# Attention on one core in steps of two heads, with four context rows weighted on TensorE in each step

## The chip, the cores and the metric

The kernel runs on 1 core of one Trainium2 chip. The metric is the device time of the program in microseconds (us). The engines of the core work side by side and are joined by semaphores: TensorE (PE), VectorE (DVE), ScalarE (ACT), GpSimd (POOL) and SyncE (SP).

## What is computed

The program is one inference step of two layers (`DEPTH` 2) with 128 context tokens and 512 latent tokens of width 1024, all in float32. Cut to what the change touches, a layer of the reference is:

```python
# latent tokens: 16 query heads in 4 key/value heads, keys = 512 latent + 128 cached
q, k = axial_rope(rms_norm(aq), rows), axial_rope(rms_norm(ak), rows)
p = softmax(einsum('bqkgd,bskd->bkgqs', q, [k, ctx_k]) * ATTN_SCALE)
o_att = einsum('bkgqs,bskd->bqkgd', p, [v, ctx_v])
y = (sigmoid(ga) * (o_rec @ w_branch_rec) + sigmoid(gb) * (o_att @ w_branch_att)) @ w_out
x = layer_norm(ALPHA * x + g1 * y)

# PEER: each token has 8 x 16 = 128 experts of 16384, chosen by top-k
a   = gelu(einsum('td,thkd->thk', h2, u_tab[expert]))      # 128 dot products a token
out = einsum('thk,thkd->td', gate * a, v_tab[expert])      # 128 weighted rows a token
x = layer_norm(ALPHA * x + g2 * out)
```

`o_rec` is a gated linear recurrence (HGRN) of 8 heads. Context and latent tokens go through the same layer with the same weights. The 128 context tokens are one tile, the 512 latent tokens are four.

## The kernel before

**Stages.** Each layer runs: the context pass (tile 0) up to its own PEER choice (`one_mix(ctx_tile)`); the gate projections of the latent tokens; 8 HGRN heads; the key, value and query projections; attention; `one_mix(one_tile)`, which is the branch mix, first norm and PEER choice of latent tile 1; the mix of the other three latent tiles; and PEER of the four latent tiles. Weight blocks of 2 MB come over the SP queue into the two slots of `ring`, in the fixed order of a list.

**Context PEER runs beside the latent work.** A PEER row is one expert of each of the 128 tokens, gathered from the table by an indirect DMA that POOL issues (L368): 128 partitions of 1024 floats, 512 KB. The context tile has 128 rows of `u` (dot products, L1879 on DVE, each with a sum over its 1024 products) and 128 rows of `v` (weighted sums, L1884 on DVE, into two partial sums that `merge_sums` joins). POOL issues them in order into 8 slots (`grow`); a slot is free when DVE is done with its row. `ctx_rows(count)` takes the next rows of this list wherever DVE's program calls it: 24 in the gate stage (`GATE_ROWS`), 6 in each HGRN head, one behind each of the levels 1 to 6 of 7 (`HEAD_ROWS`, called at L1987), 22 and 4 in the key and query stage, 2 in each attention unit, and what is left of the 256 inside `one_mix(one_tile)` (L1906).

**Attention** is 64 units a layer: 8 pairs of heads (`att_pair`), and in each pair the two heads by four tiles of 128 queries. Per unit PE computes scores of 128 queries and 640 keys (`score`, L1321 and L1322, from 64 partitions, since a head has 64 dimensions); DVE takes the minimum over the keys (`lowest`, L2078; the sign is turned); ACT takes the exponential with the row sum (L702); PE transposes the 640 probabilities in five blocks (`turn`, L1331); ACT copies them out (L717); PE multiplies by the values (`weigh`, L1347, five matmuls of 128 columns, the 64 value columns twice). Once a pair, POOL stages the queries (L377), PE transposes them (L1312), DVE divides by the row sums (`normalise`), and PE turns the result (L1355). In the first pair DVE also norms and rotates the second half of the query heads (`head_norm`, seven parts).

**Order.** Nothing reorders instructions: each engine runs its program as it is written, so the place of a call in the code is its place in the queue. PE waits at `claim` (L816) for a bank of PSUM or at semaphores. In the trace a float32 matmul stands as two instructions, a transpose as one.

**HGRN heads.** Each head goes through 7 levels; in each, DVE multiplies (L1625, L1626), copies, places a score by a mask (L1616) and takes a context row; PE waits for `level_ready`. Behind the levels DVE scales the gates of the next head (`decays`, L1959 and L1960).

## Time and profile before

| what | us |
|---|---|
| time, median of 3 runs (lowest, highest) | 5605.55 (5605.12, 5608.3) |
| span of the profiled execution | 5604.2 |
| PE busy | 4557.5 |
| DVE busy | 3712.8 |
| POOL busy | 2184.8 |
| ACT busy | 1424.7 |
| weighted context rows on DVE (L1884) | 318.8 |
| context dot rows on DVE (L1879) | 308.5 |

The profiled execution's span is 1.35 us below the median. Busy time is the sum of the instructions of an engine; engines overlap, so the sums say how full an engine is and not what sets the end. For that the stages are looked at one by one: a window is a stretch of the span, and its row gives the busy time of each engine in it, the TensorE clock that was granted as a share of full speed, and what the DMA engines moved. The attention of layer 0 lies from 888.70 to 1170.04 us, of layer 1 from 3671.02 to 3952.99 us, and `one_mix(one_tile)` follows each.

### The profile page before, as it was taken

Reading aid. Unit: us, or ns where it says so; the run is one execution under the profiler, and the core shown is the slowest. Engines: PE = TensorE matmul, PEld = TensorE weight load, DVE = VectorE, ACT = ScalarE, POOL = GpSimd, SP = SyncE. Lnnn points to the kernel's source line nnn. Section 1 sums busy time; section 2 is a strip of 40 time slices with the busy share of each in tenths; the row PEclk is TensorE's granted clock in tenths of the full one; section 3 lists DMA queues with packets and bytes.
Section 4 is the critical chain, followed back from the end, with each engine's and each line's share of the span. In section 5 each row is a group of like instructions: output and inputs, shape, how many; then the busy total and the mean of one; then the engine's idle time right before and its main releaser. Section 6 shows DMA issues by size and latency. Waiting matters only on the chain. (4 is left out here: it accounts for less than half of the span.)

```text
span 5604.2 us, 60591 instructions
## 1 busy us (share of the span) xinstructions
PE 4557.5 (81%) x17704; PEld 2520.6 (45%) x17704; DVE 3712.8 (66%) x7028; ACT 1424.7 (25%) x3646; POOL 2184.8 (39%) x1826
## 2 busy tenths in 40 slices
PE   7889988888676777777787999888795878777776
PEld 6556655646343322222265566556463433223222
DVE  2357768867788766754532677788677877677545
ACT  2112213411011333333321112134100113333333
POOL 0002124642656454455400121246336554444554
PEclk9999998999888999999999999989897989999999
DMA  7755336785989999999967543457869889999998
GB/s 267 266 184 194 122 131 219 255 331 215 384 318 346 421 419 418 418 421 416 383 225 275 197 163 117 175 191 254 330 243 365 326 311 421 421 419 411 421 421 345
DMA packets 296082, 1703.74 MB, mean 304 GB/s; under 512 B 33360, under 2 KB 43216, under 8 KB 175696
## 3 DMA queue, kind: packets, MB, share of 16 engines
q0 software_dynamic: 258048, 1342.29, 61.3%
q1 hardware_dynamic: 23712, 338.18, 15.8%
q10 hardware_dynamic: 14000, 19.42, 1.0%
q8 instruction: 148, 2.42, 0.2%
q14 instruction: 174, 1.43, 0.1%
HBM read 1694.52 MB, written 5.24 MB: 303 GB/s over the span
## 5 line engine op out<-in xcount | busy, mean ns | idle before, releaser
L368 POOL DMA_INDIRECT arena<-in_peer_uv,eidx x1024 | 1184.3, 1157 | 1458.7 <-POOLq L367 1195.4
L2151 DVE SCALAR_TENSOR_TENSOR arena<-arena 128x1024 f32<-128x1024 f32 x384 | 470.6, 1225 | 349.9 <-DMA arena<-in_peer_uv,eidx 338.4
L861 PE MATMUL banks<-arena 128*128 128x512 f32 x896 | 502.1, 643 | 237.7 <-PEq L1473 234.2
L411 POOL DMA_INDIRECT arena<-in_peer_uv,eidx x384 | 490.3, 1277 | 501.0 <-POOLq L410 475.7
L863 PE MATMUL banks<-arena 128*128 128x512 f32 x896 | 477.8, 616 | 0.0
L834 PE MATMUL banks<-ring,arena 128*128 128x512 f32 x864 | 383.7, 599 | 110.0 <-PEq L816 110.0
L463 ACT ACTIVATE arena<-arena 128x1 f32<-128x1 f32 (+1 forms) x772 | 156.9, 203 | 1035.4 <-ACTq L462 1033.6
L861 PEld LDWEIGHTS banks<-arena 128*128 128x128 f32 x896 | 155.3, 198 | 549.7 <-issue 549.2
L468 ACT ACTIVATE arena<-ident,arena 128x128 f32<-128x128 f32 x832 | 333.6, 401 | 234.7 <-ACTq L467 230.2
L2151 DVE SCALAR_TENSOR_TENSOR ring<-ring,arena 128x1024 f32<-128x1024 f32 x192 | 235.4, 1226 | 211.1 <-DMA ring<-in_peer_uv,eidx 209.9
L2161 DVE SCALAR_TENSOR_TENSOR arena<-arena 128x1024 f32<-128x1024 f32 x256 | 306.9, 1225 | 95.3 <-DMA arena<-in_peer_uv,eidx 80.8
L354 POOL COPY eidx<-arena 128x128 uint32<-128x128 uint32 x8 | 2.7, 338 | 939.8 <-POOLq L353 939.8
L1159 PE MATMUL banks<-hT,ring 128*128 128x512 f32 x768 | 350.4, 595 | 0.8 <-PEq L816 0.8
L1884 DVE SCALAR_TENSOR_TENSOR arena<-arena 128x1024 f32<-128x1024 f32 x256 | 318.8, 1283 | 42.8 <-DMA arena<-in_peer_uv,eidx 29.9
L1879 DVE SCALAR_TENSOR_TENSOR arena<-arena 128x1024 f32<-128x1024 f32 x256 | 308.5, 1227 | 46.8 <-DMA arena<-in_peer_uv,eidx 22.5
L411 POOL DMA_INDIRECT hT<-in_peer_uv,eidx x192 | 233.3, 1215 | 267.3 <-POOLq L410 251.0
L411 POOL DMA_INDIRECT ring<-in_peer_uv,eidx x192 | 261.1, 1360 | 176.4 <-POOLq L410 151.6
L861 PE MATMUL banks<-hT,arena 128*128 128x512 f32 x384 | 215.3, 643 | 140.7 <-PEq L1473 140.1
L2151 DVE SCALAR_TENSOR_TENSOR hT<-hT,arena 128x1024 f32<-128x1024 f32 x192 | 235.4, 1226 | 136.9 <-DMA hT<-in_peer_uv,eidx 127.6
L834 PE MATMUL banks<-ring,hT 128*128 128x512 f32 x672 | 304.9, 614 | 22.1 <-PEq L816 20.0
L834 PEld LDWEIGHTS banks<-ring,arena 128*128 128x128 f32 x864 | 161.9, 191 | 321.6 <-issue 321.5
L863 PEld LDWEIGHTS banks<-arena 128*128 128x128 f32 x896 | 177.8, 198 | 229.1 <-issue 229.1
(303 smaller groups left out, 7763.1 us busy)
## 6 DMA issues: line engine op xcount, KB each, us to landing
ring<-in_wblk SPq DMA_DIRECT2D x160, 2048.0 KB
arena<-in_peer_uv,eidx POOLq DMA_INDIRECT x1408
arena<-in_lnrows ACTq DMA_DIRECT2D x6, 1024.0 KB, 9.5
arena<-in_sk ACTq DMA_DIRECT2D x4, 1024.0 KB, 7.4
hT<-in_peer_uv,eidx POOLq DMA_INDIRECT x192
ring<-in_peer_uv,eidx POOLq DMA_INDIRECT x192
x<-in_x_sample ACTq DMA_DIRECT2D x1, 2048.0 KB, 28.6
out<-arena ACTq DMA_DIRECT2D x4, 512.0 KB, 7.5
```

The source lines that it names most:

```text
L368: nc.gpsimd.indirect_dma_start(grow[j], None, ins["peer_uv"], bass.IndirectOffsetOnAxis(ap=eidx[:, n, r:r + 1].bitcast(U32), axis=0)).then ...
L411: nc.gpsimd.indirect_dma_start(gslot[j], None, ins["peer_uv"].rearrange("(e h) d -> e (h d)", h=2), bass.IndirectOffsetOnAxis(ap=eidx[:, n ...
L463: return nc.scalar.activation(av[:, first:last], av[:, first:last], ACT.Gelu)
L468: nc.scalar.activation(diag[n], ident[:], ACT.Copy, scale=weight).then_inc(diag_ready, 1)
L834: last = nc.tensor.matmul(banks[:, b, :], lhs[:, k, t * P:(t + 1) * P], ring[:, s, k, :], start=k == 0, stop=k == KD - 1)
L861: nc.tensor.matmul(banks[:, b, :], diag[n], row[:, 0:CB], start=start, stop=stop, skip_group_check=True).then_inc(diag_used, 1)
L863: nc.tensor.matmul(banks[:, b + 1, :], diag[n], row[:, CB:D], start=start, stop=stop, skip_group_check=True).then_inc(free, 1)
L1159: last = nc.tensor.matmul(banks[:, 4 + c, :], ring[:, s, k, c * P:(c + 1) * P], hT[:, k, :], start=k == 0, stop=k == KD - 1)
L1879: V.scalar_tensor_tensor(grow[j], grow[j], 1.0, h2c, ALU.mult, ALU.mult, accum_out=av[:, r:r + 1]).then_inc(row_free[j], 1)
L1884: V.scalar_tensor_tensor(sums[r % 2], grow[j], wv[:, r - SLOTS:r - SLOTS + 1], sums[r % 2], ALU.mult, ALU.add).then_inc(row_free[j], 1)
L2151: V.scalar_tensor_tensor(u, u, 1.0, h2[:, t - 2, :], ALU.mult, ALU.mult, accum_out=av[:, r:r + 1])
L2161: V.scalar_tensor_tensor(grow[j], grow[j], 1.0, h2c, ALU.mult, ALU.mult, accum_out=av[:, r:r + 1]).then_inc(row_free[j], 1)
```

## The change

**Attention steps.** A step `n` is a pair of heads and one tile of 128 queries; there are 32 a layer. Both heads' scores lie in banks 0 to 3, one operation takes the minimum of both (a 128x2x640 view), and the probabilities of both are turned in three portions of 4, 4 and 2 blocks through bank 4. `weigh` puts the values first and the probabilities second, so that the result comes out turned, in two tiles of 64 columns of the array; two more matmuls spread the reciprocals of the row sums, and one multiplication (L2236) finishes the step. POOL's staging of queries is gone; PE turns one query block in each step.

**Context rows on TensorE.** The weighted sums of context rows (L1884 and `merge_sums`) are gone from DVE. In step `n` PE runs `ctx_group(n)`: four rows, each a matmul of 32 stationary columns with 512 moving columns for each half of the row, in the four column tiles of the array, 8 matmuls in all, with sums in banks 6 and 7. For this the context tokens are laid out anew: partition 32a+t and row 32j+q hold another expert of the tokens than before, so the expert numbers, gates and `h2c` are permuted by small copies (`ctx_ids`, 16 a half on DVE; 16 on ACT at the start of the key and query stage) and by `replicate` (8 times four DMAs on ACT's queue). DVE makes the diagonal weights of 16 rows in one multiplication (`spread_weights`, 128x512, 8 a layer).

**Rows and slots.** Dot rows have 6 slots (3 from row 96 on), weighted rows 7, of which four are in ring slot 1; POOL issues in each step first dot rows, then four weighted rows. SP holds the next load into ring slot 1 until PE has run group 31. Dot rows: 16 in the gate stage, 7 in a head (one behind level 0 too), 22 and 4, and 30 in the first 13 steps. `one_mix(one_tile)` has no row left.

**Smaller moves.** The scaling in `decays` moves to ACT (`keys_in`). The norm of the second query half goes in two batches of 4 heads, in steps 0 to 6 and 9 to 15, one part in a step. Gelu comes in two halves.

Core of the diff:

```diff
-GATE_ROWS = 24
-HEAD_ROWS = 6
+GATE_ROWS = 16
+HEAD_ROWS = 7
-UNIT_ROWS = 2
+STEP_ROWS = [3] + [2] * 6 + [3] * 2 + [2] * 3 + [3]
+DOT_SLOTS, LATE_SLOTS, SUM_SLOTS = 6, 3, [3, 4, 5, 12, 13, 14, 15]
...
+                    if n == len(CTX_BLOCKS + LAT_BLOCKS) + 1:
+                        assert n % 2 == 1
+                        sp.wait_ge(ring_given, 1)
+                        sp.sem_inc(ring_given, -1)
                     load(n % 2, l * NB + b)
...
+            def ctx_rows_in():
+                dot_rows(0, dots_end + LATE_SLOTS)
+                pool.wait_ge(ring_idle, 1)
+                pool.sem_inc(ring_idle, -1)
+                sum_rows(0, len(SUM_SLOTS))
+                dots, sums = dots_end + LATE_SLOTS, len(SUM_SLOTS)
+                for n in range(1, STEPS):
+                    last = min(SLOTS, dots_by(n) + LATE_SLOTS)
+                    dot_rows(dots, last)
+                    dots, last = last, min(SLOTS, len(SUM_SLOTS) + REPS * n)
+                    sum_rows(sums, last)
+                    sums = last
...
+                def ctx_group(q):
+
+                    if q % BUILD == 0:
+                        pe.wait_ge(blocks_ready, 1)
+                        pe.sem_inc(blocks_ready, -1)
+                    weights = blocks[q // BUILD % 2].rearrange("p (q j t) -> p q j t", q=BUILD, j=REPS)
+                    for j in range(REPS):
+                        r = REPS * q + j
+                        pe.wait_ge(row_full[row_slot(1, r)], landed[l, 1, r])
+                    for half in range(2):
+                        for j in range(REPS):
+                            slot = row_slot(1, REPS * q + j)
+                            op = nc.tensor.matmul(banks[32 * j:32 * j + 32, 6 + half, :], weights[:, q % BUILD, j, :],
+                                                  row_buf[slot][:, half * CB:(half + 1) * CB],
+                                                  start=q == 0, stop=q == QG - 1, skip_group_check=True)
+                            if half:
+                                op.then_inc(row_free[slot], 1)
...
+                for n in range(STEPS):
+                    for half in range(2):
+                        pe.wait_ge(prob_ready[half], 1)
+                        pe.sem_inc(prob_ready[half], -1)
+                    turn(n, 0, 4)
+                    if n + 1 < STEPS:
+                        score(n + 1)
+                    turn(n, 4, 8)
+                    if n:
+                        weigh(n - 1)
+                    if n + LT in (4 * LT, 6 * LT):
+                        pe.wait_ge(qn_ready, 1)
+                        pe.sem_inc(qn_ready, -1)
+                    turn(n, 8, 10)
+                    ctx_group(n)
+                pe.drain().then_inc(ring_given, 1)
...
-                        if tl is one_tile:
-                            ctx_rows((2 * SLOTS - jobs["at"] + 3 - n) // (4 - n))
...
-                        V.tensor_scalar(keys, keys, omlb[:, n:n + 1], None, ALU.mult)
-                        V.tensor_scalar(keep, keep, omlb[:, n:n + 1], lbf[:, n:n + 1], ALU.mult, ALU.add)
...
+                    V.tensor_reduce(low[n % 2], both_scores, AX.X, ALU.min).then_inc(low_ready[0], 1)
...
+                for n in range(STEPS):
+                    if n + 1 < STEPS:
+                        lowest(n + 1)
+                    invert(n)
+                    if n:
+                        finish(n - 1)
```

On PE, before, a unit is L1331 (turn), L1321 and L1322 (score) and L1347 (weigh); in unit 5 of the first pair L1312, which turns the next pair's queries, stands between:

```order
L1331 MATMUL banks<-ident,arena 128x128 x5
L1321 MATMUL banks<-arena 128x512
L1322 MATMUL banks<-arena 128x128
L1312 MATMUL banks<-ident,arena 128x128 x4
L1347 MATMUL banks<-arena 128x128 x5
```

And one step of the changed kernel, the second (L1433 turns, L1423 and L1425 score, L1450 weighs, L1455 spreads reciprocals, L1436 turns queries, L1472 is the context group, with rows in `arena` or `ring`):

```order
L1433 MATMUL banks<-ident,arena 128x128 x4
L1423 MATMUL banks<-arena 128x512 x2
L1425 MATMUL banks<-arena 128x128 x2
L1433 MATMUL banks<-ident,arena 128x128 x4
L1450 MATMUL banks<-arena 64x128 x10
L1455 MATMUL banks<-ident,small 64x128 x2
L1433 MATMUL banks<-ident,arena 128x128 x2
L1436 MATMUL banks<-ident,arena 128x128
L1472 MATMUL banks<-ring,arena 32x512 x3
L1472 MATMUL banks<-arena 32x512
L1472 MATMUL banks<-ring,arena 32x512 x3
L1472 MATMUL banks<-arena 32x512
```

What moved: two units' work stands in one row of the queue, the values are now the stationary side in 64 columns, and eight matmuls on gathered rows stand at the end of each step, so that the turn of the next step is queued behind the arrival of four rows.

On DVE, around a part of the norm of the second query batch (steps 11 to 12), the changed kernel reads (L1989 dot rows, L2223 minimum, L2229 reciprocal, L2236 finish, L2191 the norm's gain):

```order
L1989 SCALAR_TENSOR_TENSOR arena<-arena 128x1024 x2
L2223 TENSOR_REDUCE small<-banks 128x2
L2229 RECIPROCAL small<-small 128x2
L2236 TENSOR_TENSOR arena<-banks,arena 128x128
L2191 TENSOR_TENSOR arena<-arena,rows_g 128x4x256
L1989 SCALAR_TENSOR_TENSOR arena<-arena 128x1024 x3
L2223 TENSOR_REDUCE small<-banks 128x2
L2229 RECIPROCAL small<-small 128x2
L2236 TENSOR_TENSOR arena<-banks,arena 128x128
```

Before, at the same gain (L2050, for 8 heads at once), with the minimum of one unit (L2078) between dot rows (L1879):

```order
L2050 TENSOR_TENSOR arena<-arena,rows_g 128x4x512
L1879 SCALAR_TENSOR_TENSOR arena<-arena 128x1024 x2
L2078 TENSOR_REDUCE small<-banks 128x1
L2054 TENSOR_TENSOR arena<-arena,cos 128x32x32
L2055 TENSOR_TENSOR arena<-arena,sin 128x32x32
L1879 SCALAR_TENSOR_TENSOR arena<-arena 128x1024 x2
```

What moved: one minimum serves 2 to 3 rows where each two rows had one, the norm comes in half sizes, and each step's dot rows stand behind its minimum, finish and norm part. Where step 13 and later have nothing else, DVE before had two rows of L1884 in each unit.

On POOL the first layer's context rows were one list with the staging copies (L377) in between:

```order
L354 COPY eidx<-arena 128x2x64
L368 DMA arena<-in_peer_uv,eidx 128x1024 x42
L377 COPY arena<-arena 128x512 x2
L368 DMA arena<-in_peer_uv,eidx 128x1024 x16
L377 COPY arena<-arena 128x512
```

In the changed kernel, from the end of the head rows on:

```order
L426 DMA arena<-in_peer_uv,eidx 128x1024 x40
L426 DMA ring<-in_peer_uv,eidx 128x1024 x4
L426 DMA arena<-in_peer_uv,eidx 128x1024 x6
L426 DMA ring<-in_peer_uv,eidx 128x1024
L426 DMA arena<-in_peer_uv,eidx 128x1024 x2
L426 DMA ring<-in_peer_uv,eidx 128x1024 x3
```

What moved: dot rows and weighted rows now alternate in one queue, and the weighted rows of a step stand behind the dot rows of the same step.

## Rows read from the trace of the kernel before

**Rows 1.** The page: busy time by engine, and the group of weighted rows.

```profile
PE 4557.5 (81%) x17704; PEld 2520.6 (45%) x17704; DVE 3712.8 (66%) x7028; ACT 1424.7 (25%) x3646; POOL 2184.8 (39%) x1826
...
L1884 DVE SCALAR_TENSOR_TENSOR arena<-arena 128x1024 f32<-128x1024 f32 x256 | 318.8, 1283 | 42.8 <-DMA arena<-in_peer_uv,eidx 29.9
```

**Rows 2.** Windows: stretch, length, then the columns of the first line.

```profile
core 0: us, PE busy (x) PEld busy (x) DVE busy (x) ACT busy (x) POOL busy (x), PEclk, DMA share, GB/s
...
233.91:325.30 91.39, 77.44 (x218) 35.76 (x217) 15.70 (x24) 9.74 (x15) 0.00 (x0) 0.98 0.71 266
...
455.41:819.70 364.29, 339.21 (x1756) 228.18 (x1757) 270.33 (x530) 70.59 (x103) 58.36 (x49) 0.99 0.36 121
...
888.70:1170.04 281.34, 240.65 (x1281) 179.26 (x1281) 227.86 (x257) 112.62 (x215) 154.98 (x131) 0.87 0.70 233
890.30:950.00 59.70, 47.67 (x202) 34.06 (x203) 50.41 (x67) 22.14 (x41) 25.86 (x20) 0.73 0.49 158
1170.04:1277.19 107.15, 87.07 (x232) 40.64 (x233) 61.23 (x58) 10.91 (x17) 26.96 (x26) 0.88 0.88 352
3671.02:3952.99 281.97, 240.70 (x1281) 179.29 (x1281) 226.88 (x257) 112.84 (x215) 153.66 (x130) 0.88 0.69 230
3952.99:4059.85 106.86, 83.68 (x232) 39.39 (x233) 61.43 (x58) 10.91 (x17) 28.00 (x26) 0.92 0.90 360
```

**Rows 3.** Timeline in attention: start, us, engine line op, shape, count, [idle before <-releaser].

```profile
1062.31 0.71 PE L1331 MATMUL banks<-ident,arena 128*128 128x128 f32 x5
1062.95 1.12 PE L1321 MATMUL banks<-arena 64*128 64x512 f32 x2
...
1063.91 0.38 PE L1322 MATMUL banks<-arena 64*128 64x128 f32 x2
...
1064.22 1.38 PE L1347 MATMUL banks<-arena 128*128 128x128 f32 x10
...
1064.63 0.82 DVE L2078 TENSOR_REDUCE small<-banks 128x1 f32<-128x640 f32 x1
...
1065.54 2.48 DVE L1884 SCALAR_TENSOR_TENSOR arena<-arena 128x1024 f32<-128x1024 f32 x2
1065.57 0.79 ACT L702 ACTIVATE arena<-banks,small 128x640 f32<-128x640 f32 x1 [1.74 <-issue]
...
1074.86 0.94 PE L1331 MATMUL banks<-ident,arena 128*128 128x128 f32 x5 [2.60 <-PEq L816]
1075.72 2.07 PE L1321 MATMUL banks<-arena 64*128 64x512 f32 x2
```

**Rows 4.** Timeline of PE in the context pass: full tiles and 32-column tiles.

```profile
161.51 2.02 PE L945 MATMUL banks<-arena 128*128 128x128 f32 x16 [0.41 <-PEq L816]
163.46 1.93 PE L879 MATMUL banks<-ring,cond 128*2 128x128 f32 x64
...
233.91 7.03 PE L834 MATMUL banks<-ring,arena 128*128 128x512 f32 x16
```

**Rows 5.** Timeline of gathered rows: POOL's issue, and DVE's first use of a row.

```profile
1560.57 1.99 POOL L368 DMA_INDIRECT arena<-in_peer_uv,eidx  x1 [0.30 <-issue]
...
1566.52 1.23 DVE L2161 SCALAR_TENSOR_TENSOR arena<-arena 128x1024 f32<-128x1024 f32 x1 [1.33 <-DMA arena<-in_peer_uv,eidx]
...
1794.50 0.94 POOL L368 DMA_INDIRECT arena<-in_peer_uv,eidx  x1 [0.78 <-PE banks L863]
```

**Rows 6.** Timeline of DVE in an HGRN head.

```profile
511.35 1.23 DVE L1879 SCALAR_TENSOR_TENSOR arena<-arena 128x1024 f32<-128x1024 f32 x1
...
512.50 0.69 DVE L1625 TENSOR_TENSOR arena<-arena 128x512 f32<-128x512 f32 x1
...
542.92 0.54 DVE L1960 TENSOR_SCALAR arena<-arena,omlb,lbf 128x512 f32<-128x512 f32 x1
```

**Rows 7.** Timeline at the first head's start and in the key stage.

```profile
455.41 2.05 PE L1205 MATMUL banks<-arena 128*128 128x128 f32 x8 [3.26 <-PEq L816]
...
840.01 1.23 DVE L1879 SCALAR_TENSOR_TENSOR arena<-arena 128x1024 f32<-128x1024 f32 x1 [7.16 <-DMA arena<-in_peer_uv,eidx]
```

More of the change, by code:

```diff
@@ L146, in build @@
         gsum = small[:, 232:240]
-        sums = [acc, arena[:, 28416:28416 + D]]
+        ring1 = ring[:, 1].rearrange("p k n -> p (k n)")
+        row_buf = grow + grow[0:4] + [ring1[:, j * D:(j + 1) * D] for j in range(4)]
+        rep = [arena[:, 14336 + b * D:14336 + (b + 1) * D] for b in range(2)]
+        blocks = [acc[:, b * CB:(b + 1) * CB] for b in range(2)]
         modrows = arena[:, 0:4 * P]
@@ new lines, in sum_rows @@
+            def sum_rows(first, last):
+                for r in range(first, last):
+                    row_in(row_slot(1, r), 1, QG * (r % REPS) + r // REPS)
+            def ctx_rows_in():
[10 more added lines that the diff above has]
+                    sums = last
+                pool.wait_ge(reps_done, 1)
+                pool.sem_inc(reps_done, -1)
@@ new lines, in turn @@
+                def turn(n, first, last):
+                    claim(4)
+                    for c in range(first, last):
+                        half, j = divmod(c, NT)
+                        op = nc.tensor.transpose(at(4, c - first), pr[n % 2][half][:, j * P:(j + 1) * P], ident[:])
+                    if last == 2 * NT and n + LT < STEPS:
+                        p, qt = divmod(n + LT, LT)
+                        op = nc.tensor.transpose(query_bank, qkv[:, qt, p * P:(p + 1) * P], ident[:])
+                    op.then_inc(to_act[4], 1)
@@ L1391, in _ @@
+                pe.drain().then_inc(ring_given, 1)
+                weigh(STEPS - 1)
+                for half in range(2):
+                    pe.drain().then_inc(to_act[6 + half], 1)
+                for b in (0, 1, 2, 3, 5):
                     pe.sem_inc(bank_free[b], 1)
@@ L2022, in _, with head_norm @@
                 phase_barrier(dve, "dve")
-                def head_norm(c, heads, gain, part):
+                def head_norm(c, heads, gain, part, nt1, nt2):
                     n = heads * HD
```

551 lines of the change are left out of this document (308 added, 243 removed).

## The prediction

> **What bounds the kernel now.** I read the page first, then the windows by stage, then the timeline of one unit of attention. The page [rows 1] has PE at 81% of the span and DVE at 66%, but that is a mean over stages with other limits, and what a change is worth is read in its stage. The windows [rows 2] show the three stages touched. Attention takes 281.34 us in layer 0 and 281.97 in layer 1, with DVE busy for 227.86 and PE for 179 to 241. `one_mix(one_tile)` behind it takes 107.15 and 106.86, and the same work on the context tile, which has no rows beside it, 91.39. The heads take 364.29. In the timeline of attention [rows 3] the reader sees why DVE rules there: a unit is one minimum of 0.82 and two weighted rows of 2.48, together 3.3 us, while the PE work of a unit is 0.71 + 1.12 + 0.38 + 1.38, less overlaps, about 3.1. Two units, which are one step of the new kernel, cost 6.6; all 64 would be 212, and the other 70 us are the first pair, where DVE has the norm of the queries as well (59.70 us for a stretch of it, at a granted clock of 0.73).
>
> The sum is made against the profiled execution's 5604.2; the median is 1.35 higher, which I add at the end.
>
> **Attention: the engines' own work in a step.** DVE: one minimum over 1280 values. The trace has it for 640 at 0.82; two operations whose sizes differ by 512 elements differ by 0.54 (1.23 for 1024 and 0.69 for 512 [rows 6]), so 640 more cost 0.67, together 1.5. With the finish (about 0.3), a reciprocal and in every fourth step the weights of 16 rows (0.69) that is 2.0 to 2.7 from step 13 on, far from a bound. In steps 0 to 12 two or three dot rows (2.5 to 3.7) and a norm part of up to 1.2 join: 6.3 to 7.8.
>
> PE: ten transposes and one of queries, 11 x 0.142 = 1.56 (0.71 for five [rows 3]). Scores: two 64-row tiles side by side, 1.12 + 0.15 = 1.27. Weighing: ten matmuls in two 64-column tiles, five deep, 1.38, and the reciprocals 0.25. Context group: eight matmuls of 512 columns in four column tiles, so two deep. That tiles run side by side is in the trace: 64 instructions in 32-column tiles take 1.93 us, 0.030 each, where full tiles of the same columns take 2.02 for 16, 0.126 each [rows 4], fourfold. A full matmul of 512 is two instructions of 0.44 (7.03 for 16 [rows 4]), so the group is 2 x 0.88 = 1.75. Sum 6.2 us. No row has 64-wide tiles beside each other; the ends are full overlap (6.2) and none (score +1.1, weighing +1.4, reciprocals +0.1: 8.8). I take overlap, since the nearest row, the 32-column tiles, shows it whole.
>
> The chain through one step: score 1.27, minimum 1.5, two exponentials (0.79 and a 0.19 read-out each [rows 3]) 1.76 and then four transposes 0.57, with four hand-offs and ACT's copies between, about 6.7 in all. This is what a step costs if nothing else is late.
>
> **Attention: the rows' way round.** A slot of the seven comes free when PE has read the row, 1.0 to 1.75 into the group; POOL starts 0.78 later and issues for 0.94 (a case where POOL waits for PE to give a slot [rows 5]); a row issued at 1560.57 for 1.99 us is used at 1566.52, so it landed 3.96 behind the issue. The group of the next step needs the row that takes the first slot freed: 1.0 + 0.78 + 0.94 + 3.96 = 6.7, and 8.5 if the issue lasts 1.99 and the slot comes at 1.75. POOL's mean issue in attention is 154.98 / 131 = 1.18 [rows 2], and DVE, whose operations on SBUF go with the long ones, has little left from step 13 on; I take 7.0 for steps 13 to 31: 19 x 7.0 = 133.
>
> Steps 1 to 12 have a longer circle. POOL serves the dot rows of a step before its weighted rows, and a dot slot comes free behind DVE's last row, 6.5 into the step. Then 0.78, two issues of 1.2 (dot row, weighted rows ahead), the one that counts 0.94 and 3.96 of landing: 14.6; with the group's 1.75, 16.4 for two steps, 8.2 each. With POOL at 1.99 for three issues it is 18.6 or 9.3. DVE is busy here, as where POOL's 1.99 stands, so I take the upper one; and the 3 us in which PE then waits are like the 2.60 after which the same transposes take 0.94 and the score 2.07 instead of 1.12 [rows 3], the clock at half. Steps 0 and 1 bear the first weights (the gates and `spread_weights` stand in DVE's queue ahead of group 0) and an unfilled pipe: 8 and 11.6; steps 2 to 12 are 11 x 9.3 = 102. The start (query transposes, copy, score, minimum, exponentials) is 0.6 + 0.6 + 1.3 + 1.5 + 1.8 and some 3.5 of hand-offs, 9.3; the end, last weighing, finish and the copy of the sums, 4.5. Together 9.3 + 19.6 + 102 + 133 + 4.5 = 268.4, against 281.34 and 281.97: **-13 a layer, -26.6**.
>
> **one_mix(one_tile).** The rows left over leave it: 34 a layer at 1.283 [rows 1]. Its twin on the context tile is 91.39. To that I add 1.9, for the wait for the sums and the load into ring slot 1 that SP may only start behind group 31. 93.5 against 107.15 and 106.86: **-13.5 a layer, -27**. Ends: 91.4, or no gain in its first block, where the ring load (2 MB; 276 to 360 GB/s in these windows, so 6 to 7.5 us) is wholly uncovered: 99.
>
> **Heads.** One more row in each, behind level 0: 1.23 of DVE [rows 6], and PE waits for DVE in the levels. I count 1.1, 8 heads: **+8.8 a layer, +17.6**. What goes the other way, four scalings (the second is 0.54 [rows 6]) from DVE to ACT, lies where PE is dense and DVE next waits for ACT; I count nothing. Ends: 0 (the cover is as good as the row) and +1.23 x 8.
>
> **Gate stage.** Eight rows fewer end PE's wait of 3.26 at the first head [rows 7]; layer 1 has none there: **-3**. **Key stage:** DVE waits 7.16 for a row while a weight load has the queues [rows 7]; with 6 slots ahead instead of 8 two rows fewer stand ready: +2.5, less 0.85 for POOL's staging that is gone: **+3.3** for both. The small copies of `ctx_ids` and of the gates stand on DVE and ACT while PE is in its projections; 32 of about 0.1 a layer, counted at nothing, +3 if uncovered.
>
> Sum: -26.6 - 27 + 17.6 - 3 + 3.3 = -35.7; 5604.2 - 35.7 + 1.35 = **5570 us**.
>
> **The rivals.**
> *Rows never wait.* If rows land in 3 us, steps go by the chain (6.7) and by DVE in the first twelve (7.8): 9.3 + 8 + 94 + 127 + 4.5 = 243, -26 a layer more, 5518. For it: DMA engines are busy 0.70 in attention [rows 2] and have room. Against: 3.96 was measured with POOL steadily issuing.
> *64-wide tiles one after another.* Steps 13 to 31 become 9.1, earlier ones 9.8: +46 to +50 a layer, 5672. For it: no row shows them paired, and the score of one unit and of the next lie apart in the trace.
> *Slower by the rows' way round.* PE now stops in each step for a DMA; if the way round is 8.5 and the clock falls in PE's gaps in the early steps, steps 13 to 31 cost 7.9 to 8.7 and the others 10.8. At 8.7: 19 x 1.7 + 12 x 0.5 = 38 a layer, 5647. It decides from 7.9 on: there 19 x 0.94 x 2 eats the 35.7. For it: the drop behind the gap of 2.60, and 0.73 in the first pair [rows 2, 3]. Against: with PE's work at 6.2 a step of 7.0 leaves gaps under 1 us.
> *Column tiles overlap threefold only.* The group would be 8 x 0.88 / 3 = 2.35, +0.6 in each step's circle: 2 x 31 x 0.6 = +37, 5607, no change. For it: the fourfold row is for 128 moving columns with two stationary ones, not for 512. The Trainium skill, "TensorE: Matmul & The Clock Gate", Part 3 "Packing small matmuls", gives 3.07x as measured for four tiles at 512 columns; by it the group is an estimated 2.3 us, and the trace's fourfold speaks against it here. "TensorEngine Tiling (Array Packing)", "Key Properties", says that a change of tiling mode drains the engine, and each step has some six such changes; no row here shows what one costs.
> *It does not do what it says.* If the column tiles did not overlap at all, a group would be 7 us and a step 12 to 14: 5900 and more.
>
> **How the numbers follow.** Forecast (5535 to 5594) 0.44; rows never wait 0.15; threefold tiles 0.11; the rows' way round slower 0.18; 64-wide tiles apart 0.10; no overlap 0.02. 0.2%, or 11 us, is about what a measurement of this kernel can tell from no change. Faster 0.59, same 0.11, slower 0.30. A range of 5500 to 5650 leaves out the last two and a part of each end, and holds also the ends of the heads' (-17.6, +2) and the mix's terms (-4, +11).
>
> **What would show it.** In the profile of the changed kernel: attention windows of about 268 us, and in them a period of 7.0 from step 13 on with the PE wait ahead of L1472 ended by DMA; the group's eight matmuls in about 1.75; both score tiles in 1.3 and the ten of `weigh` in 1.4 (else the tile rivals); a granted clock not below 0.87; heads 373; the mix behind attention 93.5. Attention above 281 in steps 13 to 31 with waits for DMA would make the forecast wrong by the rows' way round, and a head stage of 364 by the cover.

## The result and the profile after

The changed kernel takes **5652.59 us** (median of 4 runs, 5645.84 to 5661.64) against 5605.34 for the kernel before (4 runs, 5600.48 to 5608.3): a ratio of 1.009, 95% interval 1.0071 to 1.0109. It is slower by 0.9%, where a gain of 0.6% was forecast, and lies 2.6 us above the range. The profiled execution has a span of 5643.8 us, 39.6 more than the one of before.

The page of the changed kernel, busy time by engine, which answers to [rows 1]:

```profile
PE 4500.8 (80%) x18920; PEld 2394.2 (42%) x18920; DVE 3386.6 (60%) x6824; ACT 1512.3 (27%) x3912; POOL 2124.8 (38%) x1814
```

VectorE is relieved of 326 us, as meant, GpSimd of 60 and TensorE of 57. Only ScalarE has more work than before, 88 us, and it is busy for 27% of the span. The time is longer all the same, so the loss is in waits. The windows of the changed kernel at the same marks as [rows 2] say in which stage (stretch, length, busy time by engine, granted clock, DMA share, GB/s; in layer 0 gate stage, heads, key and query stage, attention, two parts of attention, `one_mix`; then attention and `one_mix` of layer 1):

```profile
core 0: us, PE busy (x) PEld busy (x) DVE busy (x) ACT busy (x) POOL busy (x), PEclk, DMA share, GB/s
365.93:450.48 84.55, 83.32 (x242) 40.42 (x241) 71.05 (x253) 16.71 (x24) 25.11 (x24) 1.00 0.55 207
450.48:823.03 372.55, 340.02 (x1756) 229.19 (x1757) 266.75 (x516) 90.62 (x131) 65.31 (x58) 0.99 0.42 133
823.03:896.85 73.82, 64.40 (x159) 28.57 (x158) 56.94 (x76) 15.70 (x36) 33.38 (x29) 0.98 0.76 259
896.85:1208.01 311.16, 223.77 (x1889) 121.47 (x1889) 116.50 (x190) 126.94 (x297) 143.91 (x150) 0.89 0.76 261
913.15:1053.99 140.84, 88.26 (x709) 46.01 (x709) 67.86 (x111) 50.00 (x118) 73.73 (x75) 0.84 0.78 272
1053.99:1200.46 146.47, 122.05 (x1110) 68.43 (x1111) 44.08 (x74) 69.55 (x166) 68.69 (x73) 0.98 0.80 271
1208.01:1301.81 93.80, 80.75 (x232) 38.26 (x233) 17.64 (x23) 10.92 (x17) 0.00 (x0) 0.95 0.69 258
3712.24:4017.97 305.73, 229.22 (x1889) 124.16 (x1889) 116.72 (x190) 126.95 (x297) 144.63 (x151) 0.88 0.77 266
4017.97:4110.11 92.14, 79.10 (x232) 37.63 (x233) 17.63 (x23) 10.92 (x17) 0.00 (x0) 0.98 0.70 263
```

| stage | layer 0, before to after | layer 1 | forecast a layer |
|---|---|---|---|
| gate | 88.9 to 84.6: -4.3 | 91.9 to 84.7: -7.2 | -3 and 0 |
| heads | 364.3 to 372.6: +8.2 | 361.6 to 373.8: +12.2 | +8.8 |
| keys, queries | 69.0 to 73.8: +4.9 | 68.9 to 73.7: +4.8 | +1.7 |
| attention | 281.3 to 311.2: +29.8 | 282.0 to 305.7: +23.8 | -13 |
| `one_mix` | 107.2 to 93.8: -13.4 | 106.9 to 92.1: -14.7 | -13.5 |

Together +44.2; the stages that the change doesn't touch are 4.6 shorter in this execution than in the one of before. Attention alone has the wrong sign. It splits at group 12 (the fifth and sixth row of the windows): steps 1 to 12, counted from the start of one group to the start of the next, take 140.84 us, 11.7 each, with TensorE busy for 88 of the 141 us; from group 12 to 31 it is 146.47, 7.7 each (in layer 1 11.7 and 7.5).

**Where a step of 11.7 goes.** In layer 0 they come in pairs, a short one of about 9 and a long one of about 14 us; in layer 1 the pairs are less even (9 to 14 us). The timeline of the changed kernel through one pair, from the end of group 1 to the start of group 3 (start, us, engine line op, shape, count, [idle before <-releaser]; L1472 is the group, L1423 the score, L2223 the minimum, L803 the exponential, L811 ScalarE's copy of the spread reciprocals, L2236 the finish, L2187 a norm part, L1989 the dot rows, L426 GpSimd's gathers):

```profile
930.58 1.06 PE L1433 MATMUL banks<-ident,arena 128*128 128x128 f32 x4
931.56 1.13 PE L1423 MATMUL banks<-arena 64*128 64x512 f32 x4
...
933.16 1.49 DVE L2223 TENSOR_REDUCE small<-banks 128x2 f32<-128x1280 f32 x1 [7.09 <-DVEq L1619]
...
934.76 1.28 ACT L803 ACT_TABLE_LOAD   x1 [0.55 <-ACTq L802]
...
936.85 0.79 ACT L803 ACTIVATE arena<-banks,small 128x640 f32<-128x640 f32 x1
...
937.92 0.27 ACT L811 COPY arena<-banks 128x128 f32<-128x128 f32 x1 [0.19 <-ACTq L505]
938.35 0.29 DVE L2236 TENSOR_TENSOR arena<-banks,arena 128x128 f32<-128x128 f32 x1 [3.62 <-DVEq L2235]
...
938.87 1.23 DVE L2187 TENSOR_TENSOR arena<-arena,small 128x1024 f32<-128x1024 f32 x1
...
940.17 1.23 DVE L1989 SCALAR_TENSOR_TENSOR arena<-arena 128x1024 f32<-128x1024 f32 x1
...
942.22 1.14 POOL L426 DMA_INDIRECT arena<-in_peer_uv,eidx  x1 [6.15 <-POOLq L425]
...
944.90 0.94 POOL L426 DMA_INDIRECT arena<-in_peer_uv,eidx  x1 [0.30 <-POOLq L425]
...
950.59 1.07 PE L1472 MATMUL banks<-ring,arena 128*32 128x512 f32 x2 [7.11 <-DMA arena<-in_peer_uv,eidx]
```

Read it as one chain. The turn behind group 1 starts at 930.58, the score at 931.56, the minimum at 933.16. VectorE then waits 3.62 us ahead of the finish, since the finish needs ScalarE's copy L811, which stands behind both exponentials, which need the minimum. (Here 1.28 us of the wait are a table load of ScalarE ahead of the exponentials; 19 of the other 20 finishes between group 0 and group 12 of the two layers wait 2.34 or 2.35 us.) Only behind the finish and the norm part come the two dot rows, at 940.17. They free the slots for which GpSimd has waited 6.15 us; two dot rows go out at 942.22 and 943.66, and only then, at 944.90, the weighted row that group 3 needs. It is used at 950.59, and TensorE has waited 7.11 us for it. Group 3 then runs at the lower of the two clocks (granted 0.50, 1.2 GHz; group 2 had 1.00, 2.4 GHz): its instructions take 1.07 us where those of group 2 take 0.62, and the whole group 3.64 us instead of 1.92. Group 2 lies in between and hardly waits. From group 1's start at 927.01 to group 3's it is 23.6 us, for two steps.

### The profile page after: what moved, and what is told of

It reads as the page before. It is cut to its first block and busy times, and to the rows that moved or that the text cites. A ratio compares the mean times of both kernels' runs of the same rounds, so it can differ in the third digit from the quotient of the medians.

```text
span 5643.8 us, 63537 instructions
## 1 busy us (share of the span) xinstructions
PE 4500.8 (80%) x18920; PEld 2394.2 (42%) x18920; DVE 3386.6 (60%) x6824; ACT 1512.3 (27%) x3912; POOL 2124.8 (38%) x1814
## 5 line engine op out<-in xcount | busy, mean ns | idle before, releaser
L426 POOL DMA_INDIRECT arena<-in_peer_uv,eidx x880 | 983.8, 1118 | 1336.7 <-POOLq L425 1136.4
L481 POOL DMA_INDIRECT arena<-in_peer_uv,eidx x384 | 495.5, 1290 | 496.0 <-POOLq L480 473.5
L2306 DVE SCALAR_TENSOR_TENSOR arena<-arena 128x1024 f32<-128x1024 f32 x384 | 470.6, 1225 | 347.4 <-DMA arena<-in_peer_uv,eidx 337.1
L2316 DVE SCALAR_TENSOR_TENSOR arena<-arena 128x1024 f32<-128x1024 f32 x256 | 306.6, 1226 | 95.4 <-DMA arena<-in_peer_uv,eidx 88.8
L1989 DVE SCALAR_TENSOR_TENSOR arena<-arena 128x1024 f32<-128x1024 f32 x256 | 307.7, 1224 | 54.1 <-DMA arena<-in_peer_uv,eidx 33.0
L2323 DVE SCALAR_TENSOR_TENSOR arena<-arena 128x1024 f32<-128x1024 f32 x192 | 246.7, 1285 | 38.7 <-DMA arena<-in_peer_uv,eidx 22.5
```

What stands on the lines that cost most here:

```text
L426: nc.gpsimd.indirect_dma_start(row_buf[j], None, ins["peer_uv"], bass.IndirectOffsetOnAxis(ap=eidx[:, n, c:c + 1].bitcast(U32), axis=0)).t ...
L481: nc.gpsimd.indirect_dma_start(gslot[j], None, ins["peer_uv"].rearrange("(e h) d -> e (h d)", h=2), bass.IndirectOffsetOnAxis(ap=eidx[:, n ...
L1989: V.scalar_tensor_tensor(row_buf[slot], row_buf[slot], 1.0, rep[seg % 2], ALU.mult, ALU.mult, accum_out=av[:, c:c + 1]).then_inc(row_free[ ...
L2306: V.scalar_tensor_tensor(u, u, 1.0, h2[:, t - 2, :], ALU.mult, ALU.mult, accum_out=av[:, r:r + 1])
L2316: V.scalar_tensor_tensor(grow[j], grow[j], 1.0, h2c, ALU.mult, ALU.mult, accum_out=av[:, r:r + 1]).then_inc(row_free[j], 1)
L2323: V.scalar_tensor_tensor(acc, grow[j], wv[:, r:r + 1], acc, ALU.mult, ALU.add).then_inc(row_free[j], 1)
```

## Experiments

All times below are medians, and each kernel ran on the same chip as the kernel before, whose median there was 5604.85 (e1 to e4), 5614.16 (e5 to e8) or 5604.79 (e9 to e11). Since these differ by up to 9 us, kernels of different groups are compared by the ratio to the kernel before. "Early" is the mean of steps from group 0 to group 12, "late" from group 12 to group 31, layer 0 / layer 1, in the one profiled execution.

| kernel | time | ratio to before | attention | early | late |
|---|---|---|---|---|---|
| changed | 5652.6 | 1.0090 | 311.2 / 305.7 | 11.7 / 11.7 | 7.7 / 7.5 |
| e1 dots ahead of the finish | 5604.5 | 1.0008 | 292.1 / 286.6 | 9.8 / 9.6 | 7.8 / 7.6 |
| e2 24 and 6 dot rows | 5659.2 | 1.0097 | 317.3 / 305.4 | 11.7 / 11.5 | 8.0 / 7.6 |
| e3 group behind the next score | 5643.5 | 1.0071 | 307.2 / 307.4 | 10.0 / 10.1 | 8.4 / 8.2 |
| e4 weighted rows ahead on GpSimd | 5612.3 | 1.0011 | 291.0 / 293.2 | 9.9 / 9.7 | 7.9 / 8.1 |
| e5 as e1, from step 1 on | 5611.7 | 0.9995 | 292.6 / 292.2 | 10.5 / 10.5 | 7.6 / 7.6 |
| e6 no gathers of weighted rows | 5541.7 | 0.9894 | 252.5 / 252.4 | 8.1 / 8.0 | 7.0 / 7.0 |
| e7 ten slots from row 56 | 5659.4 | 1.0079 | 311.5 / 307.1 | 12.3 / 12.1 | 7.4 / 7.4 |
| e8 e5 + e4 + e7 | 5634.1 | 1.0041 | 301.5 / 299.9 | 11.0 / 10.9 | 7.7 / 7.7 |
| e9 no dot rows in attention | 5555.0 | 0.9910 | 263.5 / 260.7 | 7.7 / 7.9 | 7.7 / 7.5 |
| e10 e1 + e4 | 5644.8 | 1.0079 | 305.7 / 307.6 | 10.8 / 11.1 | 7.9 / 7.8 |
| e11 e1 + ten slots from row 77 | 5590.7 | 0.9975 | 280.0 / 283.4 | 9.6 / 10.2 | 7.3 / 7.1 |

The traces of e5 to e8 differ from those of the other changed kernels in one thing that their edits don't explain. In each of the 64 steps TensorE signals that the reciprocals are spread (L1455 in the changed kernel). In e5, e6, e7 and e8 this signal comes more than 0.6 us behind the end that the trace gives the matmul in 57, 11, 52 and 49 steps, by up to 8.0 us; in the changed kernel, e1 to e4 and e9 to e11 it never comes more than 0.03 us behind. The early steps of e7 have it too, although e7 is the changed kernel there. The four were taken on one chip, and no run tells whether the chip or something else is the cause (the trace of the kernel before has some late signals of TensorE as well). So the pace of their steps is weaker evidence than that of the others.

**e1: dot rows ahead of the finish.** My theory from the chain above; the rival was the row transfers' own time.

```diff
                     invert(n)
+                    if n < len(STEP_ROWS):
+                        ctx_rows(STEP_ROWS[n])
                     if n:
                         finish(n - 1)
...
-                    if n < len(STEP_ROWS):
-                        ctx_rows(STEP_ROWS[n])
```

> The changed kernel with one reordering on VectorE: in each attention step the dot rows stand ahead of the finish and of the norm part instead of behind them. Theory 1 (late dot slots): in steps 1 to 12 a circle of two steps runs over turn, score, minimum, the finish that waits 2.3 to 3.6 us for ScalarE's sums, norm part, dot rows, GpSimd's dot rows, weighted row, group. Then the finish wait (2.34), the finish (0.29) and the norm part (1.2) leave the circle, 3.8 of the 23.6 us of two steps: steps 1 to 12 fall from 11.7 to about 9.9 us, 22 us a layer, and the time from 5652 to about 5609. Theory 2 (the rows' own way: landing longer than 4 us beside each other, or the halved clock in the gaps): the order on VectorE changes nothing by itself, steps 1 to 12 stay at 11 to 12 us, time within 10 us of 5652. Steps 13 to 31 stay at 7.5 to 7.7 in both.

5604.48 us, ratio to the kernel before 1.0008 (0.9996 to 1.002): 48 us gone by the order of three calls on one engine, where 44 were expected. In the traces 38 of them lie in attention. The early steps fall from 11.7 to 9.7. No row, no slot and no transfer is different, so the theory stands: the dot slots came free too late. The edit takes the finish with its wait and the norm part (1.2 us) out of the circle together, so it doesn't say what each is worth. In the timeline of e1, the first dot row follows the minimum and its reciprocal at once and the finish comes behind the dot rows without a wait:

```profile
957.76 1.21 DVE L1989 SCALAR_TENSOR_TENSOR arena<-arena 128x1024 f32<-128x1024 f32 x1
...
960.99 0.29 DVE L2236 TENSOR_TENSOR arena<-banks,arena 128x128 f32<-128x128 f32 x1
```

**e4: weighted rows ahead of dot rows on GpSimd**, the same circle cut at another place.

```diff
-                    dot_rows(dots, last)
-                    dots, last = last, min(SLOTS, len(SUM_SLOTS) + REPS * n)
-                    sum_rows(sums, last)
-                    sums = last
+                    more = min(SLOTS, len(SUM_SLOTS) + REPS * n)
+                    sum_rows(sums, more)
+                    dot_rows(dots, last)
+                    dots, sums = last, more
```

> The changed kernel with one reordering on GpSimd: in each step the four weighted rows are issued ahead of the dot rows. Theory 1 (the weighted row waits behind dot rows whose slots come free late): the group's wait for its last row goes from 7 us in every second step to the 1 to 2 us of the late steps; but a dot row now stands behind four weighted rows (5 us of issues), so VectorE waits for dot rows, and I expect steps 1 to 12 at 9.5 to 10.5 instead of 11.7, time 5610 to 5640. Theory 2 (landing time of the rows): no change of the pace, 5645 to 5660.

5612.30 us, ratio 1.0011 (1.0000 to 1.0022), early steps 9.8. As expected of theory 1. Theory 2, the landing time of the rows, had no change of the pace and is out, by this run and by e1.

**e9: no dot rows in the attention steps.** The end of that line: what are the early steps without them? (`ctx_rows` sets the 30 dot products to 0, GpSimd skips their gathers.)

```diff
-                    row_in(row_slot(0, r), 0, dot_column(r))
+                    if r < dots_end:
+                        row_in(row_slot(0, r), 0, dot_column(r))
...
+                        else:
+                            V.memset(av[:, c:c + 1], 0.0)
```

> The changed kernel without the 30 dot rows of the attention steps: neither gathered nor multiplied (their dot products are set to 0, so the context tile's result is not the reference's); everything else, the weighted rows too, stays. Theory 1 (the early steps are long only by the dot rows in the circle and in GpSimd's queue): steps 1 to 12 run like the late ones, 7.6 to 8.1 (8.05 was the pace without gathers, where the norm parts and dot rows still stood on VectorE), so about 46 us a layer less, time 5560. Theory 2 (norm parts, the change of ScalarE's functions, or the slow start of the rows in the first steps hold them): above 9 in steps 1 to 12, time above 5590.

5555.02 us (2 runs); attention 263.49 us, early steps 7.7 and 7.9, where the late ones are 7.7 and 7.5. The norm parts and ScalarE's changes of function are still in them, so by themselves these cost at most 0.4 us a step, and of the 4 us by which the early steps of the changed kernel are longer nearly all come with the dot rows.

**e3: the group behind the next score.** The circle again, cut on TensorE.

```diff
                         score(n + 1)
+                    if n:
+                        ctx_group(n - 1)
                     turn(n, 4, 8)
...
-                    ctx_group(n)
+                ctx_group(STEPS - 1)
```

> The changed kernel with one reordering on TensorE: the context group of step n-1 stands behind the first turn and the score of step n, where it stood at the end of its own step, ahead of them. Theory 1 (the group's wait holds up the next score, and by it minimum, dot rows and rows): the circle of dot rows then runs over three steps instead of two, steps 1 to 12 fall from 11.7 to about 8.5 (bound by VectorE and chain), and from step 13 on the wait for rows (0.4 to 2.3 us a step) lies beside the chain: 7.6 falls to about 7.0. Together 38 + 11 us a layer, time about 5555. Theory 2 (GpSimd and the row transfers set the pace whatever is queued behind them): the late steps stay at 7.5 to 7.7, the early ones lose less than 1 us each, time 5630 to 5652.

5643.45 us, ratio 1.0071 (1.0053 to 1.0088). The time lies in theory 2's range, but the steps fit neither theory: the early ones fell to 10.0, more than theory 2 allows, but the late ones rose to 8.3, and the first group came 4.6 us later (20.9 against 16.3 us from the start of attention). That the late ones rise fits a way round of the rows that starts at the group's own place, since a group put later also frees its slots later; but TensorE then also has its turns and weighing behind a waiting group, and the run does not tell the two apart.

**e5: as e1, but step 0 left as it was.** In e1 the first group comes 3.4 us later.

```diff
                     invert(n)
+                    if 0 < n < len(STEP_ROWS):
+                        ctx_rows(STEP_ROWS[n])
                     if n:
                         finish(n - 1)
...
-                    if n < len(STEP_ROWS):
+                    if n == 0:
                         ctx_rows(STEP_ROWS[n])
```

> As e1_dots_first, but in step 0 the dot rows stay where the change has them, behind the first weights, since with them ahead the first group came 3.4 us later (19.7 against 16.3 us from the start of attention, and the first group waits for its weights). If that is so, the first group is back at 16.3 us and steps 1 to 12 stay at 9.7: time 5598. If the 3.4 us are only moved (the dot rows of step 0 then delay step 1), time 5604 as e1.

5611.66, ratio 0.9995 (0.9981 to 1.0009), which can't be told from e1's 1.0008; attention 292.6 and 292.2. The first group is back at 16.3, but steps 1 and 2 become 12.8 and 10.2, where e1 has 9.1 and 10.0: the 3.4 us look moved, not gained. This is one of the traces with late signals.

**e6: no gathers of weighted rows.** What do late steps cost when TensorE never waits for a row?

```diff
             def sum_rows(first, last):
-                for r in range(first, last):
+                for r in range(0):
...
-                    for j in range(REPS):
-                        r = REPS * q + j
-                        pe.wait_ge(row_full[row_slot(1, r)], landed[l, 1, r])
...
-                            if half:
-                                op.then_inc(row_free[slot], 1)
```

> The changed kernel without the gathers of the weighted context rows: GpSimd issues only the dot rows, and TensorE's groups read whatever is in the slots without a wait (the context tile's weighted sums are wrong by this). The group's matmuls, the weights and all dot rows stay. Theory 1 (the way round of the rows, 7.0 at best, sets the late steps, and the late dot slots the early ones through the group's wait): steps 13 to 31 fall from 7.6 to the chain, 6.3 to 6.8, and steps 1 to 12 from 11.7 to 8 to 9 (VectorE). Theory 2 (the chain turn, score, minimum, exponentials and copies is itself 7.5, and the waits for rows only fill its gaps): steps 13 to 31 stay at 7.4 to 7.6. By theory 1 the time is about 5540 to 5560, by theory 2 5575 to 5590, the early steps gaining in both.

5541.73 us, attention 252.54 and 252.40. From step 16 on, where its signals are in time, a step is 6.8 us, which is the chain; steps 1 to 12, with dot rows and norm parts on VectorE, are 8.05. Theory 1 had 6.3 to 6.8 and 8 to 9. The late pace of the changed kernel, 7.6, is thus 0.8 above the chain, and this is the rows'.

**e7: ten slots from row 56 on**, with the three that the dot rows leave free.

```diff
+MORE_FROM = 56
...
+            if part == 1 and r >= MORE_FROM:
+                return (SUM_SLOTS + [0, 1, 2])[(r - MORE_FROM) % 10]
...
-                    dots, last = last, min(SLOTS, len(SUM_SLOTS) + REPS * n)
+                    dots, last = last, min(SLOTS, (7 if 7 + REPS * n < MORE_FROM + 7 else 10) + REPS * n)
```

> The changed kernel with ten slots instead of seven for the weighted rows from row 56 on (the three slots that the dot rows leave free), so that from step 14 on GpSimd issues three rows further ahead. Theory 1 (a row's way round, slot free to landed, is 7.0 and sets the pace of steps 13 to 31): it has 10/4 instead of 7/4 steps of time, the group no longer waits, steps 15 to 31 fall from 7.6 to the chain, 6.3 to 6.8, about 14 us a layer, time 5625. Theory 2 (the chain or the DMA engines set it): 7.5 to 7.7 as before, time 5652.

5659.38 us, ratio 1.0079 (1.0048 to 1.011), no gain that the interval shows. From step 15 on no group waits for a row any more, and from step 16 on the pace is 7.1, better by 0.4 to 0.6 and not at the chain. The group itself takes longer there: 2.0 to 2.9 us in most steps instead of 1.92, with the full clock granted. A group with all four rows in `arena` in e7 and, for comparison, one in e11:

```profile
1129.87 2.78 PE L1475 MATMUL banks<-arena 128*32 128x512 f32 x16
...
1135.51 1.92 PE L1475 MATMUL banks<-arena 128*32 128x512 f32 x16
```

The step at which the depth changes takes 12.2 us in layer 0 and 9.6 in layer 1, and the early steps, in which nothing was changed, came out at 12.2 instead of 11.7. In the long step ScalarE starts its copy of the reciprocals 3.3 us late, since TensorE's signal for it comes only at 1080.17, while the trace has the matmul at 1074.18 to 1074.57:

```profile
1074.18 0.39 PE L1458 MATMUL banks<-ident,small 128*64 128x128 f32 x4
...
1080.27 0.27 ACT L814 COPY arena<-banks 128x128 f32<-128x128 f32 x1 [3.29 <-ACTq L508]
```

What held it back the trace doesn't show. The run was undecided, which is why e11 repeats it elsewhere.

**e2: 24 and 6 dot rows, as before the change.**

```diff
-GATE_ROWS = 16
-HEAD_ROWS = 7
+GATE_ROWS = 24
+HEAD_ROWS = 6
```

> The changed kernel with 24 dot rows in the gate stage and 6 in each HGRN head, as before the change, instead of 16 and 7; everything else stays. Theory 1 (the seventh row is on the path of the heads): the heads go from 372.6 and 373.8 back to 364 and 362, the gate stage from 84.6 and 84.7 up by 3 to 7; net -5 to -14 us over both layers, time 5638 to 5647. Theory 2 (the heads' growth comes from the scaling that moved to ScalarE, L721 to L723): the heads stay at 372 to 374 and the gate stage grows, so the time rises by 5 to 12 us.

5659.16 us, 6.6 more, but the ratios (1.0097, 1.008 to 1.0115, and 1.0090) can't be told apart. The stages can. The windows of gate stage and heads, layer 0:

```profile
365.03:463.10 98.07, 83.33 (x242) 40.47 (x241) 79.66 (x267) 17.02 (x24) 32.15 (x32) 0.94 0.61 234
463.10:828.13 365.03, 339.46 (x1756) 228.24 (x1757) 258.95 (x503) 90.27 (x130) 57.26 (x50) 0.99 0.39 121
```

The heads go back to 365.0 and 367.5: the seventh row costs 7.5 and 6.3 a layer, 0.8 to 0.9 a head. In layer 0 that leaves 0.7 of the 8.2 us, so ScalarE's scaling, which stays in this run, is not what lengthened the heads there; in layer 1 it leaves 5.9 of 12.2, which the scaling or another part of the change may hold. But the gate stage takes 98.1 us in both layers, where the kernel before had 88.9 and 91.9 for the same 24 rows. The slots are 6 instead of 8, and VectorE waits 12.6 us for rows there in layer 0 where it waited 8.5; that this is the cause was not tested. Theory 1 had 3 to 7 us for the stage; it is 13.5. So the heads are as theory 1 had them, and the time is not.

**e8 and e10: orders combined.**

> Three moves together: dot rows ahead of the finish from step 1 on, weighted rows ahead of dot rows on GpSimd, and ten slots from row 56 on. Theory 1: each takes off another wait (finish, queue, way round), so steps 1 to 12 fall below the 9.7 to 9.9 that either of the first two gave alone, to about 8.8, and the late ones to 6.8: 283 - 11 - 15 = about 265 us of attention, time 5555 to 5565. Theory 2 (one limit of 9.7 stands behind both reorderings, and the late pace is the chain): attention 285 to 290, time 5595 to 5605.

> Both reorderings without more slots: dot rows ahead of the finish on VectorE (e1) and weighted rows ahead of dot rows on GpSimd (e4). Each alone gave 9.6 to 9.9 in steps 1 to 12. Theory 1 (GpSimd's queue is the next limit: 2.3 dot rows and 4 weighted rows a step, at 1.24 us from start to start 7.8 us, at the long issues of up to 2 us more than 9): steps 1 to 12 stay at 9 to 9.8, time 5595 to 5610. Theory 2 (two separate waits, each of which both orders remove in part): 8.5 and 5575 to 5585.

e8 takes 5634.07 us (ratio 1.0041, 1.0024 to 1.0058) and e10 5644.83 (1.0079, 1.0063 to 1.0096), each worse than either of its reorderings alone, and neither near what a theory had. The way from group 1 to group 2 takes 18.3 to 19.0 us in all four layers of the two. In e10, GpSimd and VectorE:

```profile
922.17 0.93 POOL L426 DMA_INDIRECT arena<-in_peer_uv,eidx  x1 [22.35 <-POOLq L425]
...
933.83 1.23 DVE L1989 SCALAR_TENSOR_TENSOR arena<-arena 128x1024 f32<-128x1024 f32 x1 [8.34 <-DMA arena<-in_peer_uv,eidx]
...
936.28 0.29 DVE L2236 TENSOR_TENSOR arena<-banks,arena 128x128 f32<-128x128 f32 x1
```

Either order cuts the circle; both together close another. The dot row is now behind four weighted rows on GpSimd, so it comes late, and it stands ahead of the finish on VectorE, so the finish waits for it too (8.34 us ahead of the dot row), and the next weighing for the finish. e10, which changes nothing but the two orders, shows this by itself. It refutes my limit for GpSimd as the only one left, and my notion that waits taken off one by one add up.

**e11: e1 and ten slots, from row 77 on.**

> Dot rows ahead of the finish (e1) and ten slots for weighted rows, but only from row 77 on, away from the step where ScalarE changes to gelu, at which the switch at row 56 had a step of 12.2 us. If the late steps go to 7.15 as they did there, steps 20 to 31 gain 0.45 each, 5 us a layer, time about 5594. If the switch itself costs a long step wherever it stands, the gain is eaten: 5604 or more, with one step of 10 to 12 us near step 20.

5590.71 us, ratio to the kernel before 0.9975 (0.9966 to 0.9985): faster than both kernels, by 0.25% and 1.1%. There is no long step at the switch (6.5 and 6.2 us), and the window from group 21 to group 31 in layer 0 shows ten steps of 6.7 us with the clock at full:

```profile
1101.42:1168.52 67.10, 61.20 (x579) 34.37 (x579) 17.65 (x30) 35.28 (x88) 33.88 (x37) 1.00 0.86 308
```

TensorE is busy for 61.2 of 67.1 us, and no group behind group 21 waits for a row; layer 1 has the same 6.7. So the rows' way round set the late pace, and beyond it the chain does, at 6.7, as in e6.

## Why the prediction was wrong

**The step that failed: steps 1 to 12.** The prediction put a slot's release "behind DVE's last row, 6.5 into the step", from VectorE's own work laid end to end. Measured in the pair shown, the two dot slots come free at 941.4 and 942.5, where the step's turn starts at 930.58: 10.8 and 12.0 us. VectorE's work doesn't begin with the step but behind turn and score (2.6 us), and it is not laid end to end: the finish waits 2.3 to 3.6 us for ScalarE, whose copy stands behind two exponentials. I had the durations right and left out two waits between them. Two other terms were short: the landing, 4.7 us from the end of the issue instead of 3.96, and the group behind the long wait, 3.6 us at the lower clock instead of 1.75. One was too long: GpSimd's issues were taken at 1.99 us and took 0.94 to 1.14. (The prediction's own terms also give 19.0 for two steps and not 18.6.) In place of 9.3 it was 11.7, 27 us a layer more. e1 shows where: with finish, its wait and the norm part behind the dot rows, a step falls by 2.0 us and the kernel by 48.

**Steps 13 to 31** were said at 7.0 and are 7.7 and 7.5, 13.5 and 9.5 us a layer more. The mechanism was right, and one term of it was too small. The timeline of the changed kernel shows one way round:

```profile
1093.84 0.62 PE L1472 MATMUL banks<-ring,arena 128*32 128x512 f32 x2 [2.26 <-DMA arena<-in_peer_uv,eidx]
...
1096.53 0.94 POOL L426 DMA_INDIRECT ring<-in_peer_uv,eidx  x1 [3.65 <-POOLq L425]
...
1100.86 0.59 PE L1472 MATMUL banks<-arena 128*32 128x512 f32 x1 [0.70 <-DMA ring<-in_peer_uv,eidx]
```

It is 2.69 us from the group's start to GpSimd's issue, 0.94 for the issue and 3.39 until the next group uses the row: 7.02, one of the shortest. Over the 19 late steps of layer 0 the means are 2.86, 0.95 and 3.89, together 7.7; in layer 1 2.79, 0.98 and 3.73, together 7.5. The prediction had 1.78, 0.94 and 3.96, which is 6.7, and took 7.0. So issue and landing were right, and the first term was 1.0 to 1.1 us too small: the first slot comes free 1.9 us into the group and not 1.0, because each row is read a second time for its other half and these four matmuls stand last. The steps scatter with two of the terms: the last one varies from 3.4 to 4.8 us, and where the group itself ran at the lower clock (3.4 to 3.6 us) the first one is 4.1 to 4.3.

**The tiles were right.** The group, both score tiles and the ten matmuls of `weigh` in the changed kernel (the group's last instruction starts 1.29 us after the first and takes 0.60, 1.9 in all):

```profile
935.89 0.62 PE L1472 MATMUL banks<-arena 128*32 128x512 f32 x2 [0.45 <-DMA ring<-in_peer_uv,eidx]
...
937.22 0.60 PE L1472 MATMUL banks<-ring,arena 128*32 128x512 f32 x2
...
939.61 1.13 PE L1423 MATMUL banks<-arena 64*128 64x512 f32 x4
...
941.47 1.31 PE L1450 MATMUL banks<-arena 128*64 128x128 f32 x20
```

Four column tiles take 1.92 us for what takes 7.03 full, 3.7 times less with the end counted (said: 1.75; the threefold rival: 2.35), and 64-wide tiles overlap in pairs, in rows and in columns. So the three tile rivals are out, and the changes of tiling in each step cost nothing that can be seen in these rows.

**The rivals.** *Slower by the rows' way round* came, with 5647 against 5652.6, but that its number is so near is luck. It had the early steps at 10.8 and the late ones at 7.9 to 8.7, and priced the early ones at 0.5 us each where 10.8 less 9.3 is 1.5; with 1.5 it would have been about 5671. Measured, the early ones weigh more, 27 us a layer of about 39, through an order on VectorE which it didn't name. The clock fell where it said: 0.84 in the early stretch, where TensorE is idle for over a third of the time, 0.98 in the late one. Over all of attention it was 0.89 and 0.88, not below the 0.87 that the forecast allowed. *Rows never wait* is e6 in its effect, 252.5 us of attention where I had 243, with the late steps at 6.8 where I had 6.7.

**Other terms.** `one_mix` -13.4 and -14.7 (-13.5): right, though 91.39 and 1.9 are 93.3 and not 93.5. Heads +8.2 and +12.2 (+8.8), the row 0.8 to 0.9 a head (1.1): right in layer 0; e2 leaves 5.9 of layer 1's 12.2 unexplained by the row. Gate stage -4.3 and -7.2 (-3 and 0): for layer 1 I looked only for a wait ahead of the first head and missed that the stage as a whole was longer, 91.9. Key stage +4.9 and +4.8 (+1.7). The timeline of the changed kernel has the long stall with a longer idle, as forecast (8.12 for 7.16 in [rows 7]), and a wait that I had not costed:

```profile
843.07 1.23 DVE L1989 SCALAR_TENSOR_TENSOR arena<-arena 128x1024 f32<-128x1024 f32 x1 [8.12 <-DMA arena<-in_peer_uv,eidx]
...
865.83 0.25 DVE L2185 RECIPROCAL small<-small 128x16 f32<-128x16 f32 x1 [1.79 <-DVEq L2184]
...
876.47 1.23 DVE L1989 SCALAR_TENSOR_TENSOR arena<-arena 128x1024 f32<-128x1024 f32 x1 [1.31 <-DVEq L1987]
```

The 1.31 is the wait for `replicate`'s copies (L1987), the 1.79 the square root on ScalarE, for which the same place had 0.5 before.

**Open:** the late signals of TensorE in e5 to e8, and with them the step of 12.2 us at row 56, which e7 and e8 have (e8 in both layers, 12.3 and 12.1) and e11 doesn't at row 77; why a landing takes 3.4 us in one step and 4.8 in another; and what holds the early steps at 9.7 in e1 and e4, where without weighted gathers (e6) they take 8.05.

## What to carry to other kernels

When two streams of gathers share one in-order queue, follow each slot all the way round, over every engine's queue that stands between its use and its release: an operation that waits for another engine (here a finish of 0.29 us) costs that wait to all that stands behind it, and moving the slot's last reader ahead of it and of a norm part was worth 48 us. Place what releases a shared resource ahead of what waits. Two reorderings that each cut a circle may close a new one together, so they have to be costed and run as one change. And a slot that is read twice is free only behind the second reading: here that was 0.9 us of every way round, and with more slots TensorE no longer waited for it (e11). Putting both readings of a row next to each other was not tried.

## What the runs showed of the hardware

- TensorE in tiles: 16 instructions of 512 columns in four 32-column tiles take 1.92 us, where as many full ones take 7.03 [rows 4]; two 64-row tiles of 512 columns take 1.13 together, the same as one alone before [rows 3].
- The granted clock was 0.84 in the stretch where TensorE was busy for 88 of 141 us, 0.98 where it was 122 of 146, and 1.00 where it was 61 of 67. Behind a wait of 7.11 us the group's instructions take 1.07 instead of 0.62, behind one of 0.45 us 0.62.
- A gather of 512 KB in the changed kernel landed 3.2 to 6.1 us behind the end of its issue (the rows whose landing the trace tells), with a mean of 4.9 in the early steps and 4.5 to 4.6 in the late ones; the first row issued behind a late group reached its user after 3.4 to 4.8 us. GpSimd's issues follow each other at 1.24 us at best, and at up to 2.1 us in e1's early steps (960.09 to 962.18).
